# Experts in an order ranked on chip by count, and an expert loop over four 32-token groups with one gather and one scatter

## The reference, cut to what matters

```python
logits = tok @ w_router + b_router               # 256 x 32
top_val, top_idx = lax.top_k(logits, 4)
top_w = jax.nn.softmax(top_val, axis=-1)
# for each expert e and each token row that picked it:
hgu = tok[rows] @ w_gu[e] + b_gu[e]              # w_gu[e]: 1024 x 2048
gate = jnp.minimum(hgu[:, 0::2], 7.0)
up = jnp.clip(hgu[:, 1::2], -7.0, 7.0)
act = (up + 1.0) * (gate * jax.nn.sigmoid(1.702 * gate))
y = act @ w_down[e] + b_down[e]                  # w_down[e]: 1024 x 1024
out[row_tok] += y * wts[:, None]
```

## Time and profile before

| | before |
|---|---|
| median of 3 runs | 1428.87 us (1427.16 to 1434.74) |
| profiled execution: its time | 1430.1 us |
| profiled execution: its span | 1428.3 us |
| mean granted TensorE clock | 0.917 |
| busy: TensorE matmul / VectorE / ScalarE | 84% / 19% / 16% of the span |
| DMA | 455.98 MB, mean 319 GB/s |
| chain that ended last | TensorE 60%, DMA 34%, issue 3% |

### The profile page before, as it was taken

The page is one execution under the profiler, slowest core; times in us unless marked ns, Lnnn a source line. Parts: engine busy times, 40 slices in busy tenths (PEclk is TensorE's granted clock), DMA queues, the critical chain, the costliest instruction groups (busy, mean ns, idle before and its releaser), DMA issues.

```text
span 1428.3 us, 19043 instructions
## 1 busy us (share of the span) xinstructions
PE 1201.5 (84%) x7477; PEld 540.9 (38%) x7478; DVE 266.6 (19%) x786; ACT 230.9 (16%) x529; POOL 18.5 (1%) x26
## 2 busy tenths in 40 slices
PE   8999999999799766899999778696788797976677
PEld 4655868885433212333333122132222232312122
DVE  3335243632411100111111001010111011100001
ACT  2134423350111000111111011011011111100001
POOL 1100010000000000000000000000000000000000
PEclk9999999999799898989998989899898899988989
DMA  9933264223898999948527989989999999899993
GB/s 344 314 118 118 77 250 145 78 98 139 347 377 358 426 424 425 420 170 344 244 118 323 424 337 427 428 356 426 427 413 426 428 417 428 346 425 425 427 424 129
DMA packets 66265, 455.98 MB, mean 319 GB/s; under 512 B 7284, under 2 KB 13016, under 8 KB 33432
## 3 DMA queue, kind: packets, MB, share of 16 engines
q1 hardware_dynamic: 65528, 454.13, 77.6%
q0 software_dynamic: 256, 0.79, 0.2%
q10 hardware_dynamic: 448, 0.60, 0.1%
HBM read 454.45 MB, written 1.05 MB: 319 GB/s over the span
## 4 chain that ended last, share of the span: by engine, by line
PE 60%; DMA 34%; issue 3%; DVE 1%; ACT 1%; SPq 0%; ACTq 0%; DVEq 0%
DMA ring<-in_w_down 29%; PE bank L1005 16%; PE bank L1032 9%; PE bank L557 6%; PE bank L697 6%; DMA ring<-in_w_gu 5%; PE bank L972 4%; PE bank L980 4%; PE bank L991 2%; PE bank L606 2%; PE bank L893 2%; PE bank L859 2%; PE bank L546 1%; PE bank L583 1%; PE bank L881 1%
## 5 line engine op out<-in xcount | busy, mean ns | idle before, releaser
L1005 PE MATMUL bank<-ring,sp_ 128*32 128x512 f32 x2944 | 409.7, 688 | 134.0 <-DMA ring<-in_w_gu 80.2
L1032 PE MATMUL bank<-ring,mq 128*32 128x512 f32 x1472 | 184.5, 635 | 65.0 <-DMA ring<-in_w_down 62.6
L1005 PEld LDWEIGHTS bank<-ring,sp_ 128*32 128x32 f32 x2944 | 91.4, 119 | 372.3 <-issue 245.7
L1775 DVE TENSOR_SCALAR sp_<-bank 128x256 f32<-128x256 f32 x46 | 19.5, 425 | 858.5 <-PE bank L1005 858.5
L1032 PEld LDWEIGHTS bank<-ring,mq 128*32 128x32 f32 x1472 | 46.3, 114 | 195.5 <-issue 100.4
L972 PEld LDWEIGHTS bank<-sp_,sc 128*128 128x128 f32 x736 | 88.0, 199 | 24.3 <-issue 24.3
L972 PE MATMUL bank<-sp_,sc 128*128 128x64 f32 x736 | 91.1, 284 | 2.0 <-DVE sp_ L1758 2.0
L980 PE MATMUL bank<-mq,sp_ 128*128 128x512 f32 x184 | 86.1, 611 | 1.5 <-ACT sp_ L1363 1.5
L557 PE MATMUL bank<-ring 128*128 128x512 f32 x192 | 83.2, 592 | 0.0
L1336 ACT ACTIVATE mq<-bank 64x512 f32<-64x512 f32 x46 | 27.1, 589 | 318.6 <-PE bank L1032 318.6
L697 PE MATMUL bank<-ring 128*128 128x256 f32 x320 | 71.3, 381 | 0.0
(11 more groups left out here) (292 smaller groups left out, 818.3 us busy)
## 6 DMA issues: line engine op xcount, KB each, us to landing
ring<-in_w_gu SPq DMA_DIRECT2D x128, 2048.0 KB, 27.0
ring<-in_w_down SPq DMA_DIRECT2D x64, 2048.0 KB, 21.5
ring<-in_w_in SPq DMA_DIRECT2D x13, 2048.0 KB, 10.8
ring<-in_w_out SPq DMA_DIRECT2D x2, 2048.0 KB, 8.2
ring<-in_w_mem_kv SPq DMA_DIRECT2D x2, 1024.0 KB, 6.9
ring<-in_w_mem_kv SPq DMA_DIRECT2D x1, 2048.0 KB, 8.0
ring<-in_cmp_w_k SPq DMA_DIRECT2D x1, 2048.0 KB, 8.2
ring<-in_cmp_w_v SPq DMA_DIRECT2D x1, 2048.0 KB, 9.6
```

The costliest lines, as they stand in the source:

```text
L1005: mm = nc.tensor.matmul(BH[par][32 * s:32 * s + 32, :], xgT[:, k, 32 * par:32 * par + 32], w[:, c, 512 * s:512 * s + 512], start=k == 0, s ...
L1032: mm = nc.tensor.matmul(BG[64 * hh + 32 * two:64 * hh + 32 * two + 32, :], actT[par][:, o:o + 32], w[:, 2 * c + two, 512 * hh:512 * hh + 512],
L1775: V.tensor_scalar(gt[par], h[:, :, 0], LIMIT, None, ALU.min).then_inc(S("g_clip"), 1)
```

## The change

It does four things.

1. *Order.* After the counts are known, each expert gets a key (its count, then its number; experts 0 and 1, whose weights are already loading, come first), the number of larger keys is its place in the ranking, and the constant list SEATS turns the place into a **seat**, its position in the order of work. `idx` now also holds the expert of each seat, and SyncE loads by it (`load_round(n)`). TensorE picks slots by the seat's parity.
2. *Fours.* Groups are padded to a multiple of four: up to three experts, those at seats 3, 5 and 27, get an empty group more (`later`, `pad`).
3. *The loop.* A turn is four groups (`quad`). The gather stands at its head, with 128 columns; the scatter behind the first group adds y of the four groups before, 32 rows each. `down` accumulates even and odd rows in one place, in four strips of 256 columns. The four seats come packed in one integer.
4. *The other engines* follow: ScalarE writes y in four pieces of 32 x 256 and makes one copy of 512 columns of a gathered half; VectorE makes the one-hots with one or two operations over all four groups.

With the counts above, the seats hold the experts 0, 1, 13, 21, 8, 20, 17, 11, 7, 4, 23, 26, 24, 18, 27, 30, 9, 28, 10, 5, 22, 16, 6, 14, 19, 3, 12, 25, 15, 29, 2, 31.

The diff, cut to its core ("..." marks what is left out):

```diff
+QUAD = 4
+QUADS = ITEMS // QUAD
+PADS = (3, 5, 27)
+SEATS = [0, 1, 16, 8, 24, 12, 20, 28, 4, 22, 26, 6, 30, 10, 18, 14, 2, 3, 27, 5, 11, 19, 13, 21, 29, 23, 7, 25, 9, 15, 17, 31]
...
+    later = [sum(m > x for x in PADS) for m in range(NE + 1)]
+    add("later", np.tile(np.array(later[:NE] + later[1:], np.float32), (P, 1)))
+    add("pack", np.tile(np.float32(NE) ** np.arange(QUAD, dtype=np.float32), (P, 1)))
...
-            def load_round(e, odd, order):
-                f = sp.value_load(idx[0:1, bass.ds(e, 1)], min_val=0, max_val=ITEMS - 1)
+            def load_round(n, odd, order):
+                f = sp.value_load(idx[0:1, bass.ds(n, 1)], min_val=0, max_val=ITEMS - 1)
+                here = sp.value_load(idx[0:1, bass.ds(n + AT_ORDER, 1)], min_val=0, max_val=NE - 1)
                 if TWICE - 1 in order:
+                    ahead = sp.value_load(idx[0:1, bass.ds(n + (AT_ORDER + 1), 1)], min_val=0, max_val=NE - 1)
                     sp.wait_ge(S("brow_used"), f + 1)
-                    sp.dma_start(brow[not odd], b_gu[bass.ds(e + 1, 1), :]).then_inc(brow_in[not odd], 16)
+                    sp.dma_start(brow[not odd], b_gu[bass.ds(ahead, 1), :]).then_inc(brow_in[not odd], 16)
                 for q in order:
                     if q < 4:
                     else:
                         sp.wait_ge(S("down_done"), f * 2 + (q - 3))
                     if q < TWICE:
-                        load_chunk(sp, e + 1, q, not odd)
+                        load_chunk(sp, ahead, q, not odd)
                     else:
-                        load_chunk(sp, e, q, odd)
+                        load_chunk(sp, here, q, odd)
...
+            pe.wait_ge(S("seats_ready"), 1)
+            b = begin("first")
+            done(nc.tensor.matmul(b[0:NE, 0:2 * NE + 1], nit.to_broadcast([NE, NE]), AA, start=True, stop=True), "first")
...
-            def gather():
+            def gather(j, first):
+                pe.wait_ge(S("G_ready"), j + 1)
                 for half, b in ((0, BX), (1, BG)):
+                    if half and not first:
+                        pe.wait_ge(S("y_evac"), j * QUAD - 1)
                     for c in range(4):
                         for t in range(NT):
                             o = P * (4 * half + c)
-                            mm = nc.tensor.matmul(b[:, 64 * c:64 * c + 64], x2[:, t, o:o + P], Gm[:, t, :],
-                                                  start=t == 0, stop=t == NT - 1)
+                            mm = nc.tensor.matmul(b[:, P * c:P * c + P], x2[:, t, o:o + P],
+                                                  Gm[:, t].rearrange("p g n -> p (g n)"), start=t == 0, stop=t == NT - 1)
...
-            def down(i, e, par):
-                pe.wait_ge(S("a_evac"), i + 1)
+            def down(done_before, e, n):
+                pe.wait_ge(S("a_evac"), done_before + 1)
                 for d in range(2):
                     pe.wait_ge(w_full[4 + d], e * 16 + 16 * (TRUNK_TURNS + 1))
                     w = ring[:, 4 + d, :].rearrange("p (c n) -> p c n", c=4)
                     for c in range(2):
                         for two in range(2):
                             o = P * two + 32 * (2 * d + c)
-                            for hh in range(2):
-                                mm = nc.tensor.matmul(BG[64 * hh + 32 * two:64 * hh + 32 * two + 32, :], actT[par][:, o:o + 32],
-                                                      w[:, 2 * c + two, 512 * hh:512 * hh + 512],
-                                                      start=d + c == 0, stop=d + c == 2, skip_group_check=True)
+                            for s in range(4):
+                                mm = nc.tensor.matmul(BG[32 * s:32 * s + 32, 0:256], actT[n % 2][:, o:o + 32],
+                                                      w[:, 2 * c + two, 256 * s:256 * s + 256],
+                                                      start=d + c + two == 0, stop=d + c + two == 3, skip_group_check=True)
                     mm.then_inc(S("down_done"), 1)
...
+            def quad(j, first=False):
+                pack = pe.value_load(idx[0:1, bass.ds(j + AT_PACK, 1)], min_val=0, max_val=NE ** QUAD - 1)
+                at_seat = [(pack >> (5 * n)) & 31 for n in range(QUAD)]
                 if not first:
+                    seat_before = pe.value_load(idx[0:1, bass.ds(j + (AT_PACK - 1), 1)], min_val=0, max_val=NE ** QUAD - 1) >> 15
+                gather(j, first)
+                def group(n, row):
+                    if n == 0:
+                        pe.wait_ge(S("g_evac"), j * 2 + 1)
+                    up(0, at_seat[n], n, row)
+                    bias(n % 2, row)
+                    if n > 0:
+                        turn(j * QUAD + (n - 1), n - 1)
+                    elif not first:
+                        turn(j * QUAD - 1, QUAD - 1, j - 1)
+                    up(1, at_seat[n], n, row)
+                    if n == 0:
+                        pe.wait_ge(S("g_evac"), j * 2 + 2)
+                    if n > 1:
+                        pe.wait_ge(S("y_evac"), j * QUAD + (n - 1))
+                    if n > 0:
+                        down(j * QUAD + (n - 1), at_seat[n - 1], n - 1)
+                    elif not first:
+                        down(j * QUAD - 1, seat_before, QUAD - 1)
+                    up(2, at_seat[n], n, row)
+                    up(3, at_seat[n], n, row)
+                for n in range(QUAD):
+                    with pe.If((at_seat[n] & 1) > 0):
+                        group(n, 1)
+                    with pe.Else():
+                        group(n, 0)
+                    if n == 0 and not first:
+                        pe.wait_ge(S("y_evac"), j * QUAD)
+                        pe.wait_ge(S("st_evac"), j)
+                        scatter()
...
+                for s in range(4):
+                    ins = nc.scalar.activation(y_sb[32 * n:32 * n + 32, 256 * s:256 * s + 256], BG[32 * s:32 * s + 32, 0:256],
+                                               ACT.Copy)
...
+            V.scalar_tensor_tensor(out=keyrow, in0=count_row, scalar=float(NE), in1=C("key")[0:NE, :], op0=ALU.mult, op1=ALU.add)
+            V.tensor_scalar(cntc, C("full")[0:NE, :], count, None, ALU.is_lt)
+            step(V.scalar_tensor_tensor(out=keycol, in0=count, scalar=float(NE), in1=C("keycol")[0:NE, :], op0=ALU.mult, op1=ALU.add))
+            V.tensor_reduce(nit, cntc, AX.X, ALU.add)
+            step(V.tensor_scalar(over, keyrow, keycol, None, ALU.is_gt))
+            V.tensor_scalar(nit, nit, 1.0, None, ALU.add)
+            step(V.tensor_reduce(place, over, AX.X, ALU.add))
+            n32 = C("iota")[0:NE, 0:NE]
+            step(V.scalar_tensor_tensor(out=over, in0=n32, scalar=place, in1=C("seat")[0:NE, :], op0=ALU.is_equal, op1=ALU.mult))
+            step(V.tensor_reduce(seat, over, AX.X, ALU.add))
+            V.tensor_scalar(AA[:, 0:NE], n32, seat, None, ALU.is_gt)
+            step(V.tensor_scalar(AA[:, NE:2 * NE], n32, seat, None, ALU.is_ge), "seats_ready")
...
+            def slot_of(j):
+                return rank_it[:, :, bass.ds(j * QUAD, QUAD)].unsqueeze(3).to_broadcast([P, NT, QUAD, SLOT_TOK])
+            def slots():
+                return C("slots").unsqueeze(1).unsqueeze(1).to_broadcast([P, NT, QUAD, SLOT_TOK])
+            def onehot(j):
+                V.tensor_tensor(Gm, slots(), slot_of(j), ALU.is_equal).then_inc(S("G_ready"), 1)
+            def weighted(j):
+                V.tensor_tensor(Gw, slots(), slot_of(j), ALU.is_equal).then_inc(S("Gw_made"), 1)
+                dve.wait_ge(S("Gw_made"), j + 1)
+                w = w_it[:, :, bass.ds(j * QUAD, QUAD)].unsqueeze(3).to_broadcast([P, NT, QUAD, SLOT_TOK])
+                V.tensor_tensor(Gw, Gw, w, ALU.mult).then_inc(S("Gw_ready"), 1)
```

More of the change, by code:

```diff
@@ L1091, in _ @@
             pe.wait_ge(S("x2_ready"), 2)
-            gather()
             pe.wait_ge(S("idx_ready"), 1)
-            last_pair = pe.value_load(idx[0:1, NE + 2 * ITEMS:], min_val=NE // 2 - 1, max_val=ITEMS // 2 - 1)
-            pair(0, first=True)
-            with pe.Fori(1, last_pair) as j:
-                pair(j)
+            last_quad = pe.value_load(idx[0:1, AT_LAST:], min_val=NE // QUAD - 1, max_val=QUADS - 1)
+            quad(0, first=True)
+            with pe.Fori(1, last_quad + 1) as j:
+                quad(j)
@@ new lines, in _ @@
+            step_read(V.scalar_tensor_tensor(out=starts, in0=C("later")[0:NE, :], scalar=pad, in1=bank("first")[0:NE, 0:2 * NE],
+                                             op0=ALU.min, op1=ALU.add), "first")
+            step(V.tensor_tensor(picked, starts.rearrange("p (a n) -> p a n", a=2), mid(Hs, 2), ALU.mult))
+            step(V.tensor_reduce(ends, picked, AX.X, ALU.add))
+            k = C("iota")[0:NE, 0:ITEMS]
+            step(V.tensor_scalar(Eit, k, first, None, ALU.is_ge))
+            V.tensor_scalar(Ait, k, first, -float(SLOT_TOK), ALU.subtract, ALU.mult)
@@ L1721, in _ @@
```

(7 more changed lines are left out.)

289 lines of the change are left out of this document (116 added, 173 removed).

## The result

The change makes the kernel slower: 1455.2 us (median of 4 runs, 1451.48 to 1459.03) against 1429.6 on the same chip, a ratio of **1.0174, 95% interval 1.0135 to 1.0213**. The prediction was 1365 us, range 1340 to 1405. The profiled execution took 1459.03 us with a span of 1457.2.

The account below looks back on a forecast made before the run. The expert loop was taken as bound by weight transfers, with 112 us of channel idle where heavy experts keep TensorE busy. Start 398.2, transfers 893.6, idle 60, tail 12, 1.8 outside, less 1.2, gave 1365 us; range 1340 to 1405.

Parts of the forecast that it names:

- (d): Turn of the loop: 9.1 us in all, of it 1.0 us (nothing to 7.0) for refetching the longer body.
- rival A: The loop turn costs nothing extra: no refetch, loads hidden, clock kept; a turn is 4.2 us, total 1350 us; chance 0.20.
- Low clock: Behind the loop turn's wait, TensorE's lower clock costs 3.0 us (0, or 3.3 if the whole gather runs slow).
- (b): Gather and scatter once for four groups, twelve of each instead of 23; a 128-column gather takes 3.8 us, at most 4.2.
- (c): Down in strips of 256 columns: 64 records take 3.4 us per group, upper end 5.4.
- pace: TensorE's time per group of 32 tokens in the loop: 12.0 us, up to 14.
- Rival B: Narrow strips of down cost 84 ns per record: group 13.7 us, channel idle 77 us, total 1384 us; chance 0.13.
- (f): Routing ahead of the loop: more small VectorE operations and register loads delay the start by 4 us, 2 to 8.
- (a): Ranked order of experts: a light expert behind nearly each heavy one returns up to 17 us; 48 groups in 12 turns.
- rival E: The order doesn't separate heavy experts 6 to 9; still about 1370 to 1390 us, the body doing most; chance 0.04.
- Tail: The stretch after the last weights at the kernel's end: shrinks from 28.8 to 12 us.
- rival D: Each jump in the loop waits x for code: 1423 us at x = 4, slower from 4.7, 1442 at 5; chance 0.07.

Follow-up runs that it names:

- e3: The kernel before, with its own loop over pairs, but with the change's ranked order of experts: 1391.4 us, ratio 0.9721.
- e10: e9 with the experts in natural order: 1369.8 us, ratio 0.9562.
- e9: e1 with down again as 16 calls of 512 columns and a scatter for each two groups, one gather for four kept: 1365.5 us, ratio 0.9538.
- e12: e9 with turn and down back inside the parity variants of two of the four groups: 1425.1 us, ratio 0.9950.
- e11: e9 with turn and down back inside the parity variants of every group: 1421.4 us, ratio 0.9944.
- e4: e1 with the experts in natural order: 1428.4 us, ratio 0.9982.
- e1: The change with turn and down taken outside the two parity variants of each group, same order and calls: 1393.8 us, ratio 0.9724.

## Why the prediction was wrong, point by point

| version | order | counted length | packets | us |
|---|---|---|---|---|
| before | natural, pairs | 982 | 24 | 1430 |
| e3 | ranked, pairs | about 980 | 24 | 1391 |
| e10 | natural, four | 1624 | 26 | 1370 |
| e9 | ranked, four | 1624 | 26 | 1365.5 |
| e12 | ranked, four | 1753 | 109 | 1425 |
| e11 | ranked, four | 1875 | 117 | 1421 |
| e4 | natural, four | about 1860 | 118 | 1428 |
| e1 | ranked, four | 1860 | 118 | 1394 |
| after | ranked, four | 2365 | 141 | 1455 |

e11 and e9 do the same work and differ in the length of the code and in having one branch a group instead of three; e1 and the change have other strips of down and one scatter a turn less.

- **The step that failed is (d), its refetch term.** I took 1.0 us for a turn, the packet's own time, "as TensorE's sequencer stays ahead of the array for the rest". The instruction queue did show the refetch, as the last part of the prediction asked, but TensorE waited 154 us at 36 places, 4.3 us each; in the loop that is 13 us in each of 11 turns. The upper bound, 7.0 us, was set on a single wait, yet there were three in a turn. The error in the sum was to place one wait at the jump back alone. Of the rest 60 us stood behind forward jumps in the turn, over an unused variant of some 280 counted instructions, and 22 us in straight code shortly behind the jump back, which neither the forecast nor a rival had. e1, with turn and down outside the variants, has the waits at the jump back and next to none elsewhere (0.3 us). That it is the length of the jump which decides was not shown: within their turns e11 waited 12 us in all and e12 37, with equally long variants in four and in two of the groups.
- **Low clock, also (d):** 3.0 us were taken; the gather takes 5.3 to 6.8 us behind the ten waits at the jump back, 6.1 on average, and 3.84 without a wait (455.40), so it is 2.3, and 2.9 at most. In e9, where TensorE does not wait, the gather stays at 3.84 and the register loads cost nothing visible. So without a refetch the turn would be 3.8 us and 0.35 for the turned Gw, not the 9.1 of the forecast, which is rival A's condition.
- **(b) gather** 3.8 us: 3.84. **(c) down** 3.4 us, **pace** 12.0: 3.46 and 11.9. Rival B is out: where nothing interrupts them, 64 records of 128x256 cost the lower bound.
- **(f) routing** +4 us: the loop's first transfer leaves at 395.99 instead of 394.24, +1.8, just under the lower bound of 2. TensorE's first up starts at 391.88 instead of 388.93.

```profile
386.16 5.79 PE L1002 MATMUL bank<-sp_,sc 128*128 128x128 f32 x32 [5.48 <-issue]
391.88 1.92 PE L1035 MATMUL bank<-ring,sp_ 128*32 128x512 f32 x16
```

- **(a) order:** it separates, and rival E is wrong in its condition. Its last sentence, that the body does most of the work and not the order, was half right. The two are no sum: order alone gives 39 us (e3), the kept body alone 61 (e10), both together 65 (e9). Both take idle time from the same channel, and what one has filled the other can't fill again; that this is the reason was argued and not tested.
- **Tail** 12 us: 16.7 in the change, 14.6 in e9 (last weights at 1352, span 1366.6), against 28.8.
- **The sum itself** came true in the version whose code is kept. e9's windows show what was forecast for the change:

```profile
392.00:600.00 208.00, 185.85 (x1444) 60.34 (x1436) 25.52 (x64) 29.72 (x60) 0.00 (x0) 0.96 0.99 414
600.00:760.00 160.00, 121.69 (x812) 33.99 (x812) 14.73 (x37) 15.92 (x33) 0.00 (x0) 0.88 0.94 394
760.00:1352.00 592.00, 475.73 (x3396) 147.35 (x3400) 59.83 (x150) 70.09 (x145) 0.00 (x0) 0.91 0.94 396
```

  that is 6 + 12 + 43 = 62 us of channel idle, by the sum before rounding, against 60 forecast. That 1365.5 meets the forecast of 1365 to the microsecond is luck: e9's turn is cheaper than the 9.1 us and it has a second scatter in each turn, so its parts are not the forecast's one by one.
- **What happened is rival D,** given 0.07. Its mechanism (jumps over unused variants and the jump back wait for code) and its sign are as measured, but for the waits in straight code. Its price is not: it let each of five jumps in a turn wait, where about three did, and put the point from which the change is slower at 4.7 us a jump. At the mean wait of 4.3 us its formula gives 1429, no change, and about 118 us of idle channel (its terms add up to 18 us for each us of x, not the 19 it states), where 1455 and 145 were measured. It too was short by 26 us, and why was not tested; its sum has no low clock behind the waits within a turn. The reason held against D, that the first pass of today's loop keeps its pace while packets come, was weak: that pass has no jump back behind it, and its body is later kept. The evidence for D stood in the prediction, the 16 KB packets and a body 2.4 times as long, and should have moved the refetch term from its lower to its upper end.

The Trainium skill (Runtime: NRT & Kernel Launch, Instruction fetch mechanics) gives TensorE 128 KiB, or 2048 instructions, and says that a taken branch whose target is not in the current window of two 16 KiB pages waits for a fetch. In kind the runs agree: the change waits behind jumps and before doesn't. In size they agree with neither figure: the loops of 982 and 1624 counted instructions, more than the 512 of two such pages, fetched nothing between their first turn and the end of the loop, and loops of 1753 to 1875, under 2048, fetched 8 to 9 packets in every turn. The measurement decides: in this kernel 1624 were kept and 1753 not. By the page's figure of 64 bytes for an instruction (128 KiB for 2048) that is 102 and 110 KiB, an estimate.

Left open: why exactly the limit lies there; which of the places in a turn wait (in e11 and e12 too some stand in straight code behind the gather); whether the place of the loop's head within a block of 16 KB matters (no run moved it on purpose); and why e11 takes 28 us more than e1, though they are as long. They wait about the same at the jump back, 5.8 and 5.6 us. But e11 waits 12 us more within its turns and has a second scatter in each of eleven turns, at 3.7 us some 41 us of TensorE. A version of e1 that is kept was not run, so what the refetch costs e1 is not known; the 28 us between e1 and e9 are not that cost.

## What to carry to other kernels

Before unrolling a loop body or putting work inside both variants of a branch, count the instructions that the loop really runs over all its turns on the busiest engine, and look for packets on the instruction queue between its turns: none means that the code is kept. Past the limit the jump back waited 4.5 to 7.6 us in every turn of this kernel, and the change's forward jumps waited as well: in natural order the body that is kept gained 61 us (e10), the one past the limit 2 (e4). Put into variants only what differs between them; and when two edits cure the same idle resource, do not add their gains.

## What the runs showed of the hardware

- The limit is a step. From 1624 to 1753 counted instructions in the loop, packets went from 26 to 109 and the time up by 60 us; from there to 1875 nothing more was lost. With longer variants it gets worse again: from e1 (1860) to the change (2365) another 61 us were lost, within the turns.
- Code that is never run costs nothing but the jump: 1360 skipped instructions in a body of 2345 gave 25 packets and the same time as 720, 1447 us. The first jump over them waited 9 us, the later ones some 0.3 us more than without the block.
- A wait for code was 4.3 us on average and up to 7.7 in the changed kernel, for packets whose own time is about 1 us (113 in 0.8% of 16 x 915 us). That it is so long because the weights' transfers fill the channel was not tested: no run took that traffic away. The queue itself is nearly idle: 0.7% of the engines' span. A share of busy time shows nothing of such a cost; the idle time that the profile puts down to issue does, behind the jumps and in the first up behind the gather.
- A wait of 4.9 to 7.6 us cost again by the clock: the next 32 records of the gather took 5.3 to 6.8 us for 3.84, in all ten turns.
